# A two-block transformer forward pass on one core: the opening stages in another order

## The chip, the core and the metric

The kernel runs on one core of a Trainium2 chip. TensorE (PE) multiplies matrices into PSUM, VectorE (DVE) and ScalarE (ACT) read PSUM and on-chip memory (SBUF), GpSimd (POOL) reads and writes SBUF alone, and SyncE (SP) issues the DMAs. Each engine runs its own instructions in order and waits on semaphores for the others. The metric is the device time of one execution, in microseconds (us).

## The reference, cut to what matters

The reference computes four transformer layers on x (256 tokens by 1024 features). The first uses differential attention together with an attention over 256 rows of `mem`; the second uses block attention and again an attention over `mem`; two layers of another kind (stick-breaking and forgetting attention, with convolutional feed-forwards) follow. The change touches only the opening: the normalised memory times its key and value weights, and the first layer's projection of x.

```python
def _rmsnorm(x, g):
    y = x * lax.rsqrt(jnp.mean(x * x, axis=-1, keepdims=True) + EPS)
    return y * g
# layer a
z  = _rmsnorm(x, a_norm_attn) @ a_w_in           # v, q, k and the memory's queries
kv = _rmsnorm(mem, a_mem_norm) @ a_w_mem_kv      # mem_a: keys and values, 512 wide
# layer b
kv = _rmsnorm(mem, b_mem_norm) @ b_w_mem_kv      # mem_b: the same memory, other gain and weights
```

The scale of a row, rsqrt(mean square), is the same for mem_a and mem_b. It commutes with the product, so the kernel multiplies by the gain before the matmul and by the scale after it.

## The kernel before, in words

Every product is done at float32 accuracy from two float32r parts of each operand, a high and a low one, with three matmuls: high by high, low by high, high by low. Weights come in units of 128 by 1024 floats (512 KB), through four slots of `raw`. For each unit SP loads the slot, ACT writes its high part (`split`, line 815), DVE its low part (`split`, line 1128), and PE then does 24 matmuls of 256 columns or 12 of 512. SP may load a slot again when DVE has split it; ACT may write a slot's high part again when PE is done with its unit. The operand (x or memory) gets its high part from ACT (`high`, line 819) and its low part from DVE (`low`, line 1172), in eight pieces.

The mean square of an operand is made of eight squares on ACT (`squared`, line 827, two buffers in turn), eight additions on POOL (line 1497), a product with a matrix of ones on PE (`mean_square`, line 544; with `columns` also lines 549 to 550), and a logarithm and an exponential on ACT (`norm_scale`, lines 901 to 905). A square waits until POOL has taken the one two before it. `MS_AFTER` names the unit behind which PE and ACT place it.

The head of the kernel has these stages, in PE's order: matmuls on zeros that keep PE busy (`keep_warm`, line 559; each float32 one counts as two in the records); the four units of `mem_a` (keys and values of layer a's memory) into PSUM banks 0 to 3; the six units of `values("in_a")`, four of width 512 (group 0, banks 0 and 1) and two of width 256 (group 1, banks 2 and 3); the transposes of the two memory value tiles (line 568); and `fused("in_a")`, in which each projected tile (line 467) alternates with attention. In PE's order the mean square of the memory stands behind the third unit of mem_a, that of x behind the third unit of in_a. `mem_b`'s four units run at the end of the fused stage, from an operand that is made at the start (`h2_hi`, `h2_lo`).

On DVE, `take` (line 1164) multiplies mem_a's tiles by the scale as it moves them from PSUM to `ZM`; it comes behind the low parts of mem_a, three splits, the low parts of mem_b and of x, and the fourth split. `values("in_a")` on PE waits until these tiles are out (line 437), and for all nine constants (line 695). On SP the constants and `w_f` (the weights of a gate of the last layer) are issued between x and the first unit of in_a (lines 415 to 418).

Of the kernel before, what the change touches and what calls it, by code (L numbers as in the profile page):

```python
# [22 lines left out]
P = 128  # L23
D = 1024
TOK = 256
# [87 lines left out]
def build_program(nc, ins, out):  # L113
# [6 lines left out]
    with ctx:  # L120
# [52 lines left out]
        with ExitStack() as mlp:  # L173
# [36 lines left out]
        mem_in = sem("mem_in")  # L210
# [9 lines left out]
        rstd_kept = sem("rstd_kept")  # L220
# [56 lines left out]
        OPERANDS = {"mem_a": (0, 1), "mem_b": (8, 1), "in_a": (16, 1), "up_a": (24, 1), "in_b": (32, 2),  # L277
# [8 lines left out]
            ["mem_a", "in_a", "up_a", "in_b", "up_b", "final", "in_sb", "post_sb", "up_sb", "post_ffn_sb",  # L286
# [3 lines left out]
        MS_AFTER = {"mem_a": 2, "in_a": 2, "up_a": 1, "in_b": 2, "up_b": 1, "in_sb": 3, "up_sb": 2, "in_fox": 3,  # L290
# [80 lines left out]
        def _(sp):  # L371
            sp.dma_start(gains[:], ins["gains"]).then_inc(mem_in, 16)
            sp.dma_start(ZM[:], ins["mem"]).then_inc(mem_in, 16)
# [26 lines left out]
            for name in order:  # L400
                g = plan[name]
                nk, body = len(g["ks"]), g["body"]
                if nk == 1 and any(g["unit"] <= unit < g["unit"] + g["units"] for unit in rotations):
                    for s in range(g["units"]):
                        unit = g["unit"] + s
                        load(g, s, 0, unit - RING + 1, s % RING)
                        if unit in rotations:
                            rotate(*rotations[unit])
                elif g["trips"] == 1:
                    for s in range(body):  # L410
                        load(g, s, 0, g["unit"] + s - RING + 1 if g["unit"] else None, s % RING)
                    if name == "mem_a":
                        sp.dma_start(ones[:], ins["ones"]).then_inc(ones_in, 16)
                        sp.dma_start(X[:], ins["x"]).then_inc(x_in, 16)
                        for dst, const in CONSTS:
                            sp.dma_start(dst[:], ins[const]).then_inc(consts_in, 16)
                        sp.dma_start(H[:, 0:KT // 2, :].rearrange("p a (b c) -> p (a b) c", c=P),
                                     ins["w_f"]).then_inc(wf_in, 16)
# [11 lines left out]
        def _(pe):  # L430
            n_ms, n_vt = [0], [0]

            def values(name):
# [3 lines left out]
                pe.wait_ge(tile_out, g["tile"])  # L437
                for s, (group, _, width, k_tiles) in enumerate(value_units(name)):
                    pe.wait_ge(lo_ready, g["unit"] + s + 1)
# [12 lines left out]
                    if s == MS_AFTER[name]:  # L452
                        mean_square(columns=True)

# [238 lines left out]
            keep_warm(log_ms, 20)  # L693
            gemm("mem_a", a_hi, a_lo)
            pe.wait_ge(consts_in, 16 * len(CONSTS))
            values("in_a")
            transpose_values(ZM, 2, 2)

# [101 lines left out]
        def _(act):  # L800
# [91 lines left out]
            def norm_scale(columns=False):  # L892

                act.wait_ge(ms_done, n_norm[0] + 1)
                if n_norm[0] == NORMS["in_a"]:
                    act.wait_ge(tile_out, plan["in_a"]["tile"])
                    act.wait_ge(rstd_kept, 1)
# [7 lines left out]
                nc.scalar.activation(rstd[:], log_ms[:], ACT.Exp, scale=-0.5).then_inc(rstd_ready, 1)  # L905
# [13 lines left out]

            def values(name, middle=None):  # L920
# [3 lines left out]
                for s, (group, first, width, k_tiles) in enumerate(units):  # L924
                    split(0, RING, g["unit"] + s + RING, KT)
                    if s == MS_AFTER[name]:
                        norm_scale(columns=True)
                    if k_tiles.stop == KT:
# [120 lines left out]
            act.wait_ge(mem_in, 32)  # L1049
            for k in range(KT):  # L1050
                high("mem_a", ZM, a_hi, 0, 0, k)
            for u in range(RING):
                split(0, RING, u, KT)
                for k in (2 * u, 2 * u + 1):
                    squared("mem_a", ZM[:, k, :], 0, 0, k)
                    high("mem_b", ZM, h2_hi, 0, 0, k)
# [4 lines left out]
            project("mem_a", middle=norm_scale)  # L1061
            for k in range(KT):
                squared("in_a", X[:, k, :], 0, 0, k)
# [48 lines left out]
        def _(dve):  # L1112
# [24 lines left out]
            def query_key_tile(name, s):  # L1137
# [7 lines left out]
                if memory >= 0:  # L1145
                    dve.wait_ge(rstd_kept, 1)
# [4 lines left out]
            def values(name):  # L1151

                g = plan[name]
                for s in range(g["values"]):
                    split(0, RING, g["unit"] + s + RING - 1, KT)

            def take(name, norm, dst, shift=0):

                per = plan[name]["body"]

                def tile(i, done, b, first):
                    dve.wait_ge(units_done, done)
                    dve.wait_ge(rstd_ready, NORMS[norm] + 1)
# [526 lines left out]
```

## Time and profile before

| what | value |
|---|---|
| time, median of 3 runs | 1336.09 us (1330.67 to 1338.53) |
| the profiled execution: its own time | 1337.67 us |
| the profiled execution: its span | 1335.9 us |
| mean granted clock of TensorE | 0.966 of full speed |
| PE busy | 1246.4 us (93%) |
| DVE, ACT, POOL busy | 947.2, 734.2, 477.9 us |

### The profile page before, as it was taken

The numbers are of one execution on the slowest core, as the hardware profiler recorded it, in microseconds if no ns is written. First come the engines' busy times: TensorE is split into PE (matmuls) and PEld (weight loads), VectorE is DVE, ScalarE is ACT, GpSimd is POOL, SyncE is SP. The second block draws the span as 40 slices with busy tenths as digits, with TensorE's granted clock in tenths as the row PEclk, the third lists the DMA queues.
The fourth block names the chain that finished last, engine by engine and source line by source line (L and its number), as shares of the span: only waits on it lengthen the run. The fifth ranks groups of instructions, "written<-read, shape, count | busy, mean of one in ns | idle before, by whom it ended". The sixth has DMA issues, their size and how long they took to land. (4 is left out here: it accounts for less than half of the span.)

```text
span 1335.9 us, 29554 instructions
## 1 busy us (share of the span) xinstructions
PE 1246.4 (93%) x9952; PEld 1177.5 (88%) x9952; DVE 947.2 (71%) x1545; ACT 734.2 (55%) x1307; POOL 477.9 (36%) x465
## 2 busy tenths in 40 slices
PE   7988999999997999999997889998999999899896
PEld 7977999999985999999885779998979978899896
DVE  6598677656597677545699479997475756899844
ACT  6556554444554555444656566665465556666642
POOL 2231255300022355210222258885130004888711
PEclk9999899999998999999998799999989989999998
DMA  7544365566543456656443225555645433555472
GB/s 273 174 143 127 111 205 189 178 196 204 177 142 96 157 189 192 202 188 190 157 127 111 82 93 179 173 182 151 186 136 174 127 95 112 158 181 171 141 207 85
DMA packets 63287, 212.40 MB, mean 159 GB/s; under 512 B 7793, under 2 KB 8945, under 8 KB 62833
## 3 DMA queue, kind: packets, MB, share of 16 engines
q1 hardware_dynamic: 63216, 211.50, 50.3%
q8 instruction: 39, 0.64, 0.2%
q14 instruction: 32, 0.25, 0.1%
HBM read 207.28 MB, written 1.05 MB: 156 GB/s over the span
## 5 line engine op out<-in xcount | busy, mean ns | idle before, releaser
L1128 DVE TENSOR_TENSOR w_lo<-raw,w_hi 128x1024 fp32r<-128x1024 f32 (+2 forms) x408 | 508.9, 1253 | 144.8 <-ACT w_hi L815 144.8
L815 ACT CAST w_hi<-raw 128x1024 fp32r<-128x1024 f32 (+2 forms) x408 | 408.2, 1004 | 251.6 <-PE bank L499 166.3
L497 PE MATMUL bank<-h_hi,w_hi 128*128 128x256 f32 x1168 | 328.6, 281 | 12.2 <-DVE w_lo L1128 11.3
L498 PE MATMUL bank<-h_lo,w_hi 128*128 128x256 f32 x1168 | 324.0, 277 | 0.0
L499 PE MATMUL bank<-h_hi,w_lo 128*128 128x256 f32 x1168 | 323.9, 277 | 0.0
L1497 POOL TENSOR_TENSOR sumsq<-sumsq,square 128x256 f32<-128x256 f32 x107 | 95.6, 893 | 471.5 <-ACT square L827 287.2
L497 PE MATMUL bank<-a_hi,w_hi 128*128 128x256 f32 x896 | 251.3, 281 | 11.0 <-DVE w_lo L1128 9.3
L498 PE MATMUL bank<-a_lo,w_hi 128*128 128x256 f32 x896 | 250.5, 280 | 0.0
L499 PE MATMUL bank<-a_hi,w_lo 128*128 128x256 f32 x896 | 250.4, 279 | 0.0
L497 PEld LDWEIGHTS bank<-h_hi,w_hi 128*128 128x128 f32 x1168 | 220.2, 189 | 19.3 <-issue 18.6
L499 PEld LDWEIGHTS bank<-h_hi,w_lo 128*128 128x128 f32 x1168 | 220.4, 189 | 0.0
L498 PEld LDWEIGHTS bank<-h_lo,w_hi 128*128 128x128 f32 x1168 | 220.1, 188 | 0.1
L497 PEld LDWEIGHTS bank<-a_hi,w_hi 128*128 128x128 f32 x896 | 170.4, 190 | 12.4 <-DVE w_lo L1128 10.1
L498 PEld LDWEIGHTS bank<-a_lo,w_hi 128*128 128x128 f32 x896 | 170.4, 190 | 0.0
L499 PEld LDWEIGHTS bank<-a_hi,w_lo 128*128 128x128 f32 x896 | 169.8, 190 | 0.0
L467 PE MATMUL bank<-h_hi,w_hi 128*128 128x256 f32 x512 | 147.6, 288 | 0.0
L468 PE MATMUL bank<-h_lo,w_hi 128*128 128x256 f32 x512 | 143.3, 280 | 0.0
L469 PE MATMUL bank<-h_hi,w_lo 128*128 128x256 f32 x512 | 143.1, 280 | 0.0
L1541 POOL TENSOR_TENSOR prod<-H 128x256 f32<-128x256 f32 x64 | 89.2, 1393 | 84.8 <-DVE H L1203 84.8
L467 PEld LDWEIGHTS bank<-h_hi,w_hi 128*128 128x128 f32 x512 | 97.4, 190 | 5.1 <-issue 4.9
L1555 POOL TENSOR_TENSOR H<-H,conv_sb 128x256 f32<-128x256 f32 x88 | 97.1, 1103 | 9.8 <-DVE H L1226 7.7
L469 PEld LDWEIGHTS bank<-h_hi,w_lo 128*128 128x128 f32 x512 | 97.2, 190 | 0.0
(154 smaller groups left out, 2123.6 us busy)
## 6 DMA issues: line engine op xcount, KB each, us to landing
raw<-in_w_up_sb SPq DMA_DIRECT2D x44, 512.0 KB, 3.4
raw<-in_w_up_fox SPq DMA_DIRECT2D x44, 512.0 KB, 3.4
raw<-in_w_up_a SPq DMA_DIRECT2D x32, 512.0 KB, 3.4
raw<-in_w_down_a SPq DMA_DIRECT2D x32, 512.0 KB, 4.7
raw<-in_w_up_b SPq DMA_DIRECT2D x32, 512.0 KB, 3.4
raw<-in_w_down_b SPq DMA_DIRECT2D x32, 512.0 KB, 4.4
raw<-in_w_in_sb SPq DMA_DIRECT2D x24, 512.0 KB, 3.6
raw<-in_w_in_fox SPq DMA_DIRECT2D x24, 512.0 KB, 4.3
```

The source lines that it names most:

```text
L467: nc.tensor.matmul(dst, w_hi[:, slot, w], src_hi[:, k, :], start=k == 0, stop=False)
L468: nc.tensor.matmul(dst, w_hi[:, slot, w], src_lo[:, k, :], start=False, stop=False)
L469: last = nc.tensor.matmul(dst, w_lo[:, slot, w], src_hi[:, k, :], start=False, stop=k == KT - 1)
L497: nc.tensor.matmul(dst, w_hi[:, slot, w], src_hi[:, at + k, :], start=begin, stop=False)
L498: nc.tensor.matmul(dst, w_hi[:, slot, w], src_lo[:, at + k, :], start=False, stop=False)
L499: last = nc.tensor.matmul(dst, w_lo[:, slot, w], src_hi[:, at + k, :], start=False, stop=end)
L815: nc.scalar.copy(w_hi[:, slot, 0:k * P], raw[:, slot, 0:k * P]).then_inc(hi_ready, 1)
L1128: nc.vector.tensor_tensor(w_lo[:, slot, 0:k * P], raw[:, slot, 0:k * P], w_hi[:, slot, 0:k * P].bitcast(f32), ALU.subtract).then_inc(lo_re ...
L1497: nc.gpsimd.tensor_tensor(sumsq[:], sumsq[:], square[:, b, :], ALU.add).then_inc(sum_done, 1)
L1541: nc.gpsimd.tensor_tensor(prod[:, b % 2, :], u_buf[:, b, :], u_buf[:, b, :], ALU.mult).then_inc(prod_ready, 1)
L1555: nc.gpsimd.tensor_tensor(m_buf[:, b % 2, :], u_buf[:, b % 2, :], conv[:, layer, 0, bass.ds(i * 4 + b, 1)].broadcast_to([P, TOK]), ALU.mul ...
```

## The change

The loads: `mem` comes in two DMAs of half its pieces, with a semaphore each. The nine constants are issued behind the load of the third unit of in_a (unit 6 of the stream, s == 2), and w_f behind the fifth (s == 4), no longer ahead of the first.

ACT and DVE start on the first half of the memory alone, and split the first weight unit after six of the eight pieces. The squares of the memory and the operand of mem_b move from the start to the middle of `values("in_a")` (`opening`). The squares of x are done ahead of `values("in_a")`, between splits, and x's mean square is the first on PE, behind the second unit of in_a. The memory's mean square follows behind the fifth.

mem_a's four tiles are copied from PSUM to `Z` as they are (`take_memory`). They are multiplied by the memory's scale at the end of `values("in_a")`, from SBUF to SBUF, and PE's transposes wait for that (`mem_scaled`). `values("in_a")` on PE waits for two tiles to be out, and for four in its second group. `keep_warm` makes 16 matmuls and not 20. `norm_scale` writes the memory's scale straight to `rstd_mem`, and the copy of it goes. The new semaphores' declarations are left out here, and so are unchanged lines:

```diff
@@ -274,7 +275,7 @@
-        OPERANDS = {"mem_a": (0, 1), "mem_b": (8, 1), "in_a": (16, 1), "up_a": (24, 1), "in_b": (32, 2),
+        OPERANDS = {"mem_a": (0, 1), "in_a": (8, 1), "mem_b": (16, 1), "up_a": (24, 1), "in_b": (32, 2),
                     "q_b": (33, 2), "up_b": (48, 1), "in_sb": (56, 1), "up_sb": (64, 1), "in_fox": (72, 2),
@@ -283,11 +284,11 @@
         NORMS = {n: i for i, n in enumerate(
-            ["mem_a", "in_a", "up_a", "in_b", "up_b", "final", "in_sb", "post_sb", "up_sb", "post_ffn_sb",
+            ["in_a", "mem_a", "up_a", "in_b", "up_b", "final", "in_sb", "post_sb", "up_sb", "post_ffn_sb",
              "in_fox", "post_fox", "up_fox", "post_ffn_fox"])}
-        MS_AFTER = {"mem_a": 2, "in_a": 2, "up_a": 1, "in_b": 2, "up_b": 1, "in_sb": 3, "up_sb": 2, "in_fox": 3,
+        MS_AFTER = {"in_a": 1, "up_a": 1, "in_b": 2, "up_b": 1, "in_sb": 3, "up_sb": 2, "in_fox": 3,
                     "up_fox": 2}
@@ -369,8 +370,10 @@
         def _(sp):
-            sp.dma_start(gains[:], ins["gains"]).then_inc(mem_in, 16)
-            sp.dma_start(ZM[:], ins["mem"]).then_inc(mem_in, 16)
+            sp.dma_start(gains[:], ins["gains"]).then_inc(gains_in, 16)
+            for h in range(2):
+                part = slice(h * KT // 2, (h + 1) * KT // 2)
+                sp.dma_start(ZM[:, part, :], ins["mem"][:, part, :]).then_inc(mem_in[h], 16)
             def load(g, f, part, free, slot):
@@ -406,16 +409,18 @@
                             rotate(*rotations[unit])
+                        if name == "in_a" and s == 2:
+                            for dst, const in CONSTS:
+                                sp.dma_start(dst[:], ins[const]).then_inc(consts_in, 16)
+                        if name == "in_a" and s == 4:
+                            sp.dma_start(H[:, 0:KT // 2, :].rearrange("p a (b c) -> p (a b) c", c=P),
+                                         ins["w_f"]).then_inc(wf_in, 16)
                 elif g["trips"] == 1:
...
                         sp.dma_start(X[:], ins["x"]).then_inc(x_in, 16)
-                        for dst, const in CONSTS:
-                            sp.dma_start(dst[:], ins[const]).then_inc(consts_in, 16)
-                        sp.dma_start(H[:, 0:KT // 2, :].rearrange("p a (b c) -> p (a b) c", c=P),
-                                     ins["w_f"]).then_inc(wf_in, 16)
                 else:
@@ -434,8 +439,11 @@
                 g = plan[name]
-                pe.wait_ge(tile_out, g["tile"])
+                if name != "in_a":
+                    pe.wait_ge(tile_out, g["tile"])
                 for s, (group, _, width, k_tiles) in enumerate(value_units(name)):
+                    if name == "in_a" and k_tiles.start == 0:
+                        pe.wait_ge(tile_out, 2 * group + 2)
                     pe.wait_ge(lo_ready, g["unit"] + s + 1)
@@ -451,6 +459,8 @@
                         mean_square(columns=True)
+                    if name == "in_a" and s == 4:
+                        mean_square()
             def query_key_tile(name, s, src_hi, src_lo):
@@ -690,11 +700,13 @@
             pe.wait_ge(warm_ready, 1)
-            keep_warm(log_ms, 20)
+            keep_warm(log_ms, 16)
             gemm("mem_a", a_hi, a_lo)
...
             values("in_a")
+            pe.wait_ge(mem_scaled, 4)
             transpose_values(ZM, 2, 2)
+            pe.wait_ge(h_lo, operand_count("mem_b", 0, 0, KT - 1))
             fused("in_a", lambda s: query_key_tile("in_a", s, *((h1_hi, h1_lo) if s < 2 + 2 * ROPE_PAIRS
@@ -892,9 +904,7 @@
                 act.wait_ge(ms_done, n_norm[0] + 1)
-                if n_norm[0] == NORMS["in_a"]:
-                    act.wait_ge(tile_out, plan["in_a"]["tile"])
-                    act.wait_ge(rstd_kept, 1)
+                dst = rstd_mem if n_norm[0] == NORMS["mem_a"] else rstd
                 if columns:
@@ -902,7 +912,7 @@
                 link(nc.scalar.activation(log_ms[:], bank[7][:, 0:TOK], ACT.Ln, scale=1.0 / D, bias=eps_col[:]))
-                nc.scalar.activation(rstd[:], log_ms[:], ACT.Exp, scale=-0.5).then_inc(rstd_ready, 1)
+                nc.scalar.activation(dst[:], log_ms[:], ACT.Exp, scale=-0.5).then_inc(rstd_ready, 1)
                 n_norm[0] += 1
@@ -916,6 +926,17 @@
                     squared(norm, X[:, k, :], 0, 0, k)
+
+            def opening(s):
+
+                if s == 0:
+                    for k in range(KT):
+                        high("mem_b", ZM, h2_hi, 0, 0, k)
+                elif s in (1, 2):
+                    for k in range(4 * (s - 1), 4 * s):
+                        squared("mem_a", ZM[:, k, :], 0, 0, k)
+                elif s == 4:
+                    norm_scale()
             def values(name, middle=None):
@@ -925,6 +946,8 @@
                         norm_scale(columns=True)
+                    if name == "in_a":
+                        opening(s)
                     if k_tiles.stop == KT:
@@ -1046,21 +1069,26 @@
             nc.scalar.preload_act_table_set("natural_log_exp_and_others")
-            act.wait_ge(mem_in, 32)
-            for k in range(KT):
+            act.wait_ge(gains_in, 16)
+            act.wait_ge(mem_in[0], 16)
+            for k in range(4):
                 high("mem_a", ZM, a_hi, 0, 0, k)
-            for u in range(RING):
+            act.wait_ge(mem_in[1], 16)
+            for k in (4, 5):
+                high("mem_a", ZM, a_hi, 0, 0, k)
+            split(0, RING, 0, KT)
+            for k in (6, 7):
+                high("mem_a", ZM, a_hi, 0, 0, k)
+            for u in range(1, RING):
                 split(0, RING, u, KT)
-                for k in (2 * u, 2 * u + 1):
-                    squared("mem_a", ZM[:, k, :], 0, 0, k)
-                    high("mem_b", ZM, h2_hi, 0, 0, k)
             act.wait_ge(x_in, 16)
...
             act.wait_ge(a_ready, RING)
-            project("mem_a", middle=norm_scale)
-            for k in range(KT):
-                squared("in_a", X[:, k, :], 0, 0, k)
+            for u in range(RING):
+                for k in (2 * u, 2 * u + 1):
+                    squared("in_a", X[:, k, :], 0, 0, k)
+                split(0, RING, RING + u, KT)
             values("in_a")
@@ -1143,27 +1171,22 @@
                 if memory >= 0:
-                    dve.wait_ge(rstd_kept, 1)
                     dst, scale = ZM[:, 4 + memory, :], rstd_mem
...
                 split(0, RING, unit + RING - 1, KT)
-            def values(name):
+            def values(name, after_second=None):
                 g = plan[name]
-                for s in range(g["values"]):
+                for s in range(len(value_units(name))):
                     split(0, RING, g["unit"] + s + RING - 1, KT)
-
-            def take(name, norm, dst, shift=0):
-
-                per = plan[name]["body"]
-
-                def tile(i, done, b, first):
-                    dve.wait_ge(units_done, done)
-                    dve.wait_ge(rstd_ready, NORMS[norm] + 1)
-                    nc.vector.tensor_tensor(dst[:, i * per + (shift + b), :], bank[b][:, 0:TOK], rstd[:],
-                                            ALU.mult).then_inc(tile_out, 1)
-                return tile
+                    if s == 1 and after_second is not None:
+                        after_second()
+
+            def take_memory(u):
+
+                dve.wait_ge(units_done, u + 1)
+                nc.vector.tensor_copy(Z[:, 8 + u, :], bank[u][:, 0:TOK]).then_inc(tile_out, 1)
             def low(name, src, dst_hi, dst_lo, i, per, k):
@@ -1392,18 +1415,26 @@
             nc.vector.memset(eps_col[:], EPS).then_inc(a_ready, RING)
-            for k in range(KT):
+            for k in range(6):
                 low("mem_a", ZM, a_hi, a_lo, 0, 0, k)
-            for u in range(RING - 1):
+            split(0, RING, 0, KT)
+            for k in (6, 7):
+                low("mem_a", ZM, a_hi, a_lo, 0, 0, k)
+            for u in range(1, RING):
                 split(0, RING, u, KT)
             for k in range(KT):
-                low("mem_b", ZM, h2_hi, h2_lo, 0, 0, k)
-            for k in range(KT):
                 low("in_a", X, h1_hi, h1_lo, 0, 0, k)
-            dve.wait_ge(h_lo, 2 * KT)
-            project("mem_a", before=take("mem_a", "mem_a", ZM))
-            nc.vector.tensor_copy(rstd_mem[:], rstd[:]).then_inc(rstd_kept, 1)
-            values("in_a")
+            for u in range(RING):
+                take_memory(u)
+                if u:
+                    split(0, RING, RING - 1 + u, KT)
+            values("in_a", lambda: [low("mem_b", ZM, h2_hi, h2_lo, 0, 0, k) for k in range(KT)])
+            dve.wait_ge(rstd_ready, NORMS["mem_a"] + 1)
+            dve.wait_ge(h_lo, operand_count("mem_b", 0, 0, KT - 1))
+            dve.wait_ge(tile_out, RING)
+            dve.wait_ge(sum_done, 2 * KT)
+            for u in range(RING):
+                nc.vector.tensor_tensor(ZM[:, u, :], Z[:, 8 + u, :], rstd_mem[:], ALU.mult).then_inc(mem_scaled, 1)
             dve.wait_ge(consts_in, 16 * len(CONSTS))
@@ -1570,8 +1601,8 @@
                     trip(i, False)
+            sum_squares("in_a")
             sum_squares("mem_a")
-            sum_squares("in_a")
             pool.wait_ge(consts_in, 16 * len(CONSTS))
```

## Rows read from the trace of the kernel before

**Rows 1.** The page: busy time and share of one engine.
```profile
PE 1246.4 (93%) x9952; PEld 1177.5 (88%) x9952; DVE 947.2 (71%) x1545; ACT 734.2 (55%) x1307; POOL 477.9 (36%) x465
```

**Rows 2.** Windows of the head: stretch, length, busy of five engines, clock, DMA share, GB/s.
```profile
6.00:9.00 3.00, 3.00 (x16) 2.64 (x15) 2.17 (x6) 2.71 (x7) 0.00 (x0) 1.00 1.01 412
...
18.00:21.00 3.00, 3.00 (x27) 2.89 (x25) 3.00 (x5) 2.94 (x8) 1.86 (x3) 1.00 0.99 400
...
26.30:31.50 5.20, 4.58 (x24) 4.40 (x25) 3.80 (x8) 0.93 (x3) 0.00 (x0) 0.67 0.74 221
```

**Rows 3.** Timeline of PE: start, us, engine, line, operation, tiles, count, idle before.
```profile
1.20 11.18 PE L559 MATMUL bank<-log_ms 128*128 128x256 f32 x40 [1.20 <-DVE log_ms L1393]
12.03 0.47 PE L497 MATMUL bank<-a_hi,w_hi 128*128 128x256 f32 x1
...
20.70 0.59 PE L544 MATMUL bank<-sumsq,ones_sb 128*128 128x256 f32 x2
26.37 0.58 PE L497 MATMUL bank<-a_hi,w_hi 128*128 128x256 f32 x1 [5.08 <-DVE w_lo L1128]
...
31.51 0.47 PE L447 MATMUL bank<-w_hi,h_hi 128*128 128x512 f32 x1 [0.56 <-issue]
...
40.25 0.70 PE L544 MATMUL bank<-sumsq,ones_sb 128*128 128x256 f32 x2 [0.24 <-POOL sumsq L1497]
...
49.65 0.60 PE L568 MATMUL bank<-ident_sb,ZM 128*128 128x128 f32 x4
```

**Rows 4.** Timeline of DVE, head of the kernel.
```profile
16.82 5.19 DVE L1172 SCALAR_TENSOR_TENSOR h_lo<-ZM,gains_sb,h_hi 128x256 fp32r<-128x256 f32 x8
21.94 3.24 DVE L1172 SCALAR_TENSOR_TENSOR h_lo<-X,gains_sb,h_hi 128x256 fp32r<-128x256 f32 x8
25.11 3.48 DVE L1128 TENSOR_TENSOR w_lo<-raw,w_hi 128x1024 fp32r<-128x1024 f32 x3
```

**Rows 5.** Timeline of ACT, head of the kernel.
```profile
19.13 3.29 ACT L819 ACTIVATE h_hi<-X,gains_sb 128x256 fp32r<-128x256 f32 x8
...
38.78 2.92 ACT L815 CAST w_hi<-raw 128x1024 fp32r<-128x1024 f32 x3
41.62 0.25 ACT L901 ACTIVATE log_ms_col<-bank,eps_col 128x2 f32<-128x2 f32 x1
...
42.50 0.42 ACT L905 ACTIVATE rstd<-log_ms 128x256 f32<-128x256 f32 x1
...
45.20 1.26 ACT L932 ACTIVATE v_tok<-bank,rstd_col 128x512 f32<-128x512 f32 x2
```

**Rows 6.** Timeline of SP, issues of DMAs.
```profile
1.68 2.37 SPq L380 DMA_DIRECT2D raw<-in_w_mem_a  x4
...
4.61 0.45 SPq L414 DMA_DIRECT2D X<-in_x  x1
...
9.08 0.44 SPq L416 DMA_DIRECT2D b_f_sb<-in_b_f  x1
```

**Rows 7.** DMAs: size and time from issue to landing; the first is unit 0's.
```profile
raw<-in_w_mem_a SPq DMA_DIRECT2D x1, 512.0 KB, 5.9
X<-in_x SPq DMA_DIRECT2D x1, 1024.0 KB, 9.6
b_f_sb<-in_b_f SPq DMA_DIRECT2D x1, 0.5 KB, 10.8
```

**Rows 8.** Timeline of POOL in the head, and the additions' least, median and longest ns.
```profile
10.99 9.16 POOL L1497 TENSOR_TENSOR sumsq<-sumsq,square 128x256 f32<-128x256 f32 x8 [9.93 <-ACT square L827]
32.54 7.66 POOL L1497 TENSOR_TENSOR sumsq<-sumsq,square 128x256 f32<-128x256 f32 x8 [10.87 <-issue]
L1497 POOL TENSOR_TENSOR sumsq<-sumsq,square x16: 737/741/1539, 11.0 to 39.5; 128x256 f32<-128x256 f32 x16
```

**Rows 9.** PE's windows behind two waits of 2.1 us: stretch, length, busy, clock, DMA, GB/s.
```profile
800.00:803.00 3.00, 2.68 (x15) 0.69 0.50 153
1143.00:1146.00 3.00, 2.72 (x23) 1.00 0.53 157
```

More of the change, by code:

```diff
@@ L209, in build_program @@
         x_in = sem("x_in")
-        mem_in = sem("mem_in")
+        gains_in = sem("gains_in")
+        mem_in = [sem(f"mem_in{h}") for h in range(2)]
+        mem_scaled = sem("mem_scaled")
         raw_in = [sem(f"raw_in{s}") for s in range(RING)]
@@ L219, in build_program @@
         rstd_ready = sem("rstd_ready")
-        rstd_kept = sem("rstd_kept")
         col_ready = sem("col_ready")
```

## The prediction, made before the changed kernel had run

> **What bounds the kernel now.** The page comes first: PE is busy for 93% of the span and the next engine, DVE, for 71% [rows 1]. So the question for a change of order is which waits of PE it takes out of the chain, and which it puts in. The change ends at the transposes of the memory's values: from there on both kernels issue the same work on PE in the same order. Those transposes start at 49.65 us [rows 3], and I forecast the time by when they start afterwards.
>
> PE's own timeline shows where those 49.65 us go. PE runs matmuls on zeros until 12.03, then three units of mem_a until 20.70, which is 2.89 us a unit. After the mean square it stands idle for 5.08 us, until the fourth unit's low part is written at 26.3. It takes up that unit at 26.37 and starts the values at 31.51, behind the eviction of the scaled tiles. There the mean square of x waits only 0.24 us, and the values run on to 49.65: 9.40 us from that mean square for three units, of which it takes 0.9 itself, so 2.83 us a unit [rows 3]. DVE's timeline gives the reason for the idle time: the low parts of mem_b (5.19 us) and of x (3.24 us) stand ahead of the fourth split, which begins at 25.11 [rows 4]. A second loss hides behind it. In the window from 26.3 to 31.5 the granted clock is 0.67, so PE ran a part of it at 1.2 GHz after that idle time; 5.2 us at 0.67 are 1.7 us lost [rows 2]. Idle time, lost clock and the eviction make 7 to 8 us, and that is all that a better order can win.
>
> **The start.** Four matmuls on zeros go, eight records. In the window from 6 to 9 us 16 records take 3.00 us, 0.19 us each [rows 2], so PE is free 1.5 us earlier, at 10.5. By their mean, 11.18 us over 40 [rows 3], it would be 2.2 us. The weights have to be there: unit 0 is issued at 1.68 and lands 5.9 us later, at 7.6 [rows 6, 7]. ACT's split takes 0.97 us (a third of 2.92) [rows 5] and DVE's 1.16 us (a third of 3.48) [rows 4], so it is ready at 9.8, since six pieces of the memory are enough ahead of it. The two halves of the memory serve this. They cost SP one more issue, about 0.5 us, which its long queue hides; without that cover units 0 to 3 would come 0.5 us later. The four units then follow each other, since mem_b's operand is no longer ahead of their splits: 10.5 + 4 x 2.89 = 22.1.
>
> **The constants.** This is the new wait. PE still waits for all nine ahead of the values, and they now queue on SP and in the DMA engines behind units 4, 5 and 6. x lands at 4.61 + 9.6 = 14.2 and b_f, the last constant, at 9.08 + 10.8 = 19.9 [rows 6, 7]: the constants took 5.7 us behind x. Three units of 512 KB at 400 GB/s [rows 2] take 1.31 us each, so the last lands at 14.2 + 3.9 + 5.7 = 23.8. I take this value, since it keeps the queue in order and uses the constants' own row. The lower bound is no wait at all (22.1). The upper is the latency itself: unit 6 may be issued when unit 2 is split, near 13.1, nine issues of 0.49 us bring b_f to 17.5, and 10.8 us more give 28.3. So PE waits from 22.1 to 23.8, with everything else at hand: x's high parts are ready at 14.2 + 3.3 = 17.5 [rows 5], its low parts at 18.1, and unit 4 is split by 20.5 behind two copies of mem_a's tiles. Unscaled eviction itself costs DVE no more than before, and takes the scale off this path.
>
> **x's mean square.** Its squares and additions start at 17.5 between splits. In that form the eight additions took 9.16 us [rows 8], so they end at 27. PE wants them behind two value units, at 23.8 + 5.7 = 29.5. The wait is nothing, with 2.5 us of cover; with that gone each microsecond would be on the path. With 0.9 us for the mean square and three more units (8.5) PE comes to the memory's mean square at 38.9.
>
> **The memory's mean square.** ACT is the chain here. Unit 4 is done at 26.7, so the split of unit 8 ends at 27.6. The eight high parts of mem_b take 3.3 us (as x's did [rows 5]): 30.9. The split of unit 9 gives 31.9, x's scale, 1.3 us (41.62 to 42.92 [rows 5]), gives 33.2. Then come the squares. In the form in which POOL sets the pace, eight additions took 7.66 us, after 0.55 us for the first square [rows 8]: 41.4. The bounds are 6.1 us (eight at 0.76) and 12.3 us (eight at the longest, 1.54) [rows 8]. So PE waits from 38.9 to 41.4, 2.5 us, and everything behind it in PE's queue waits too: the sixth unit, the transposes, the first projected tile. With 0.6 us for the mean square and one unit it is through at 44.8.
>
> The Trainium skill has a rule against this part: SBUF — State Buffer, "Who interferes with whom", says that a VectorE instruction with two SBUF inputs holds up a GpSimd instruction that reads SBUF. The rows fit it, with additions between 737 and 1539 ns; by the median alone the chain would end 1.6 us earlier than by the 7.66 us, by the longest 4.6 us later (rival D).
>
> **The scaling.** The last square ends about 1.4 us ahead of the last addition, at 40.0. ACT then has a split (41.0), the eviction of the first values, 1.26 us [rows 5] (42.2), a split (43.2), and the memory's scale, 0.9 us (44.1). DVE splits until 44.4 and makes four products of 128x256 at 0.40 us, the price of x's low parts (3.24 over 8 [rows 4]): 46.0. The transposes wait for this, so they start at 46.0, 3.65 us earlier than before.
>
> **The clock.** PE waits twice for about 2 us. Behind two waits of 2.1 us later in this trace the clock was 0.69 once and 1.00 once [rows 9]. I take it that the wait of 2.5 us brings it down and that of 1.7 us doesn't. A fall costs up to 1.7 us [rows 2], but PE has 1.2 us to spare between 44.8 and 46.0, so 0.6 us are on the path.
>
> **The rest.** w_f moves behind unit 8 and is wanted by ACT only after the transposes; it costs nothing, and if it were late it would hold the fused stage's first DVE work. The order of the operands and of the norms changes counts only, and the copy of the scale (0.29 us on DVE) goes from a place that nobody waits for.
>
> **The sum.** 3.65 - 0.6 = 3.0 us less. The profiled execution took 1337.67 us, 1.8 us more than its span and 1.6 us over the median: 1334.7 for it, and 1336.09 - 3.0 = 1333.1 us by the median of the runs. Of the 7 to 8 us in the head about 4.5 come back as the waits for constants, for POOL and for the scaling.
>
> **The rivals.** A: the constants are there when PE wants them (b_f's 4 bytes a partition may have been held by w_f, which was issued right behind it and now isn't). PE starts the values 1.7 us earlier and all that follows moves with it: 1331.4; with additions at 0.76 us too it would be 1329.4. For it speaks that the other constants came sooner; against it that the queue ahead is the longer by 1.5 MB.
>
> B: the clock falls at the wait for constants as well. Then 1.7 us are lost ahead of everything: 1334.8. For it speaks the 0.69 behind 2.1 us, against it the 1.00.
>
> C, the other side: the constants are late. If b_f keeps 10.8 us from its issue, the values start at 28.3 instead of 23.8, 4.5 us later, and after a wait of 6.2 us the clock falls, as it did behind 5.08 us: 1333.1 + 4.5 + 1.7 = 1339.3. It decides from where the values start 3.0 us later than I say, at 26.8, or with the fallen clock at 25.1. Against it: 10.8 us was mostly the queue ahead, which by 17.5 is nearly empty.
>
> D: the additions for the memory run at POOL's longest. They end 4.6 us later, all on PE's path: 1337.7. Against it: DVE has only two splits in that stretch.
>
> E: the 3 us are given back later, in the fused stages where PE waits for other engines: 1336.1. For it speaks the spread of the three runs, 7.9 us, which is more than all I forecast.
>
> **How the numbers follow.** My forecast 0.40, A 0.20, B 0.14, C 0.07, D 0.06, E 0.13. A measurement of this kernel can tell about 0.5%, 6.7 us. Faster by more than that is below 1329.4: the fast end of A (0.10), and scatter around my own case (0.06), 0.16 in all. Slower by more, above 1342.8, would need C or D with scatter: 0.05. Within: 0.79. The range reaches from A's fast end, with a little scatter, to between D and C: 1328.5 to 1338.0.
>
> **What would show it.** PE's first weight matmul near 10.5; no gap between units of mem_a; a gap ahead of line 447's first matmul with a DMA of a constant as releaser, ending near 23.8; a gap of about 2.5 us ahead of the second mean square (line 544's successor), released by POOL; transposes near 46. I am wrong if PE's gaps sum to well under 4 us there (then A or better), or if the transposes come early and the total doesn't move (E).

## The result

The changed kernel takes 1329.55 us, the median of 20 runs; the kernel before takes 1333.07 us, the median of 20 runs that include its three shown above. The ratio is 0.9971, with a 95% interval of 0.9958 to 0.9984: 3.5 us less by the medians, 2.1 to 5.6 by the interval. I had forecast 3.0 us less. The forecast time, 1333.1, was made against a median of three runs that lay 3 us above the median of twenty, so it is the difference that was right.

The page of the kernel after, which answers to [rows 1]:

```profile
span 1326.3 us, 29540 instructions
...
PE 1235.6 (93%) x9944; PEld 1166.7 (88%) x9944; DVE 949.7 (72%) x1548; ACT 733.7 (55%) x1307; POOL 479.7 (36%) x465
```

PE's timeline of the kernel after, to be read against [rows 3]; the bracket is the idle time ahead and who ended it:

```profile
1.21 8.65 PE L569 MATMUL bank<-log_ms 128*128 128x256 f32 x32 [1.21 <-DVE log_ms L1416]
10.63 0.39 PE L507 MATMUL bank<-a_hi,w_hi 128*128 128x256 f32 x1 [0.78 <-DVE w_lo L1156]
...
22.25 0.50 PE L455 MATMUL bank<-w_hi,h_hi 128*128 128x512 f32 x1 [0.44 <-DMA b_f_sb<-in_b_f]
28.80 0.70 PE L554 MATMUL bank<-sumsq,ones_sb 128*128 128x256 f32 x2 [0.78 <-POOL sumsq L1528]
41.63 1.12 PE L554 MATMUL bank<-sumsq,ones_sb 128*128 128x256 f32 x2 [3.35 <-POOL sumsq L1528]
46.57 0.60 PE L578 MATMUL bank<-ident_sb,ZM 128*128 128x128 f32 x4
```

The one wait of 5.08 us is gone. The transposes start at 46.57 against 49.65 before, 3.08 us earlier (forecast: 46.0, and 0.6 for the clock). By PE's own timeline the 3.08 us are three parts: its first unit starts 1.40 us earlier; the waits between there and the transposes are 4.57 us (0.44, 0.78, 3.35) where they were 5.88 (5.08, 0.56, 0.24); and the work between takes 0.37 us less. This is an account and not a price: e12 below takes back a half of the earlier start, and the head hardly feels it.

Three timelines of the kernel after, ACT's, DVE's and POOL's, where they make the chain in front of the memory's mean square and of the transposes:

```profile
27.65 3.30 ACT L831 ACTIVATE h_hi<-ZM,gains_sb 128x256 fp32r<-128x256 f32 x8
30.85 1.03 ACT L827 CAST w_hi<-raw 128x1024 fp32r<-128x1024 f32 x1
...
33.00 0.71 ACT L839 ACTIVATE square<-ZM 128x256 f32<-128x256 f32 x2
...
43.73 0.42 ACT L915 ACTIVATE rstd_mem<-log_ms 128x256 f32<-128x256 f32 x1
```

```profile
44.50 1.43 DVE L1437 TENSOR_TENSOR ZM<-Z,rstd_mem 128x256 f32<-128x256 f32 x4
```

```profile
18.64 10.11 POOL L1528 TENSOR_TENSOR sumsq<-sumsq,square 128x256 f32<-128x256 f32 x8 [17.59 <-ACT square L839]
33.53 3.79 POOL L1528 TENSOR_TENSOR sumsq<-sumsq,square 128x256 f32<-128x256 f32 x4 [3.31 <-issue]
37.48 4.10 POOL L1528 TENSOR_TENSOR sumsq<-sumsq,square 128x256 f32<-128x256 f32 x4 [0.17 <-ACT square L839]
```

The high parts of mem_b, a split and x's scale stand ahead of the memory's first square on ACT.

The two spans differ by 9.6 us, three times what the head gives. Summed over windows of 5 us from 0 to 1315, the time lost to a clock below full, (1 - granted clock) x 5 us, is 40.9 us in the trace before and 32.5 in the one after, and 1.7 in the head of both. So 8.4 us of lost clock, of which a part fell on PE's idle time, differ after the head, where the two kernels are the same. The 20 runs of either spread over 9 to 11 us.

### The profile page after: what moved, and what is told of

It is laid out like the page before. It is cut to its first block and busy times, and to the rows that moved or that the text cites. A ratio compares the mean times of both kernels' runs of the same rounds, so it can differ in the third digit from the quotient of the medians.

```text
span 1326.3 us, 29540 instructions
## 1 busy us (share of the span) xinstructions
PE 1235.6 (93%) x9944; PEld 1166.7 (88%) x9944; DVE 949.7 (72%) x1548; ACT 733.7 (55%) x1307; POOL 479.7 (36%) x465
## 5 line engine op out<-in xcount | busy, mean ns | idle before, releaser
L509 PE MATMUL bank<-h_hi,w_lo 128*128 128x256 f32 x1168 | 323.7, 277 | 0.0
L509 PE MATMUL bank<-a_hi,w_lo 128*128 128x256 f32 x896 | 248.1, 277 | 0.0
L509 PEld LDWEIGHTS bank<-h_hi,w_lo 128*128 128x128 f32 x1168 | 219.5, 188 | 0.0
L509 PEld LDWEIGHTS bank<-a_hi,w_lo 128*128 128x128 f32 x896 | 168.9, 188 | 0.0
```

The source lines that it names most:

```text
L509: last = nc.tensor.matmul(dst, w_lo[:, slot, w], src_hi[:, at + k, :], start=False, stop=end)
```

## The experiments

A landmark serves for the head, since it stands out from the scatter of the total: ACT's first softmax exponential, in the second stage, at 64.07 us before and at 61.00 in the kernel after.

```profile
64.07 0.51 ACT L965 ACTIVATE p_buf<-s_buf,unit_bias 128x256 f32<-128x256 f32 x1 [1.38 <-DVE unit_bias L1306]
```

```profile
61.00 0.51 ACT L988 ACTIVATE p_buf<-s_buf,unit_bias 128x256 f32<-128x256 f32 x1 [1.39 <-DVE unit_bias L1329]
```

It has a scatter of its own. From the first projected tile to the landmark it is 14.07 us in the kernels before and after and in e9, and 13.66 to 13.69 in e1, e4 to e8, e11 and e12, where the code of that stretch is the same (last section). So 0.4 us of a difference between the two groups is not the edit's. "Ratio" is the ratio of the time to the kernel before's, with its 95% interval; it rests on 12 runs, or 6 for e2 and e10. e5 to e8 are one execution each, under the profiler, and have no ratio.

**e1: the changed kernel again.**

> The changed kernel once more, beside the kernel before on one chip, as the base for the others of this group. My theory (the gain is what the head gives: the transposes start 3.1 us earlier, and nothing else is different): the transposes start at 46.6 us within 0.3, and the ratio to before is near 0.997 to 0.998. Rival (most of the 9.6 us between the two profiled spans comes from the change): the ratio is near 0.993.

Ratio 0.9983 (0.9968 to 0.9997), transposes at 47.72, landmark at 61.75. The ratio is what I expected; the transposes are 1.1 us later than I gave. The constants landed 1 us later (23.2, not 22.2), but the memory's mean square moved by 0.24 us only. The rest came behind it, from the clock. Windows of PE alone (stretch, length, busy, clock, DMA share, GB/s) in the kernel after, then in e1, then in e8, in which the wait is filled:

```profile
39.00:42.00 3.00, 0.37 (x1) 0.96 0.56 175
42.00:45.00 3.00, 3.00 (x14) 0.50 0.46 124
45.00:48.00 3.00, 3.00 (x27) 0.97 0.67 228
```

```profile
39.00:42.00 3.00, 0.13 (x1) 0.75 0.54 175
42.00:45.00 3.00, 3.00 (x12) 0.50 0.37 138
45.00:48.00 3.00, 3.00 (x19) 0.61 0.60 217
```

```profile
39.00:42.00 3.00, 3.00 (x15) 1.00 0.51 175
42.00:45.00 3.00, 3.00 (x25) 1.00 0.35 117
45.00:48.00 3.00, 2.18 (x20) 1.00 0.69 232
```

**e8 and e11: the wait filled.** e8 is one execution, e11 the same kernel over 12 runs.

```diff
                     if name == "in_a" and s == 4:
+                        keep_warm(ones, 8)
                         mean_square()
```

> The changed kernel with 8 matmuls on ones (about 3.0 us) on PE just ahead of the memory's mean square, in the stretch where it waits 3.35 us. It tells what the clock's fall cost there. My theory (the sixth unit ran mostly at 1.2 GHz, 4.4 us in place of 2.83, and 1.1 of the 1.6 us were hidden by the scaling on DVE): the granted clock stays at 1.00, the sixth unit ends near 45.0, the transposes start at 45.9 to 46.1, 0.6 us earlier. Rival (PE's clock is the path there): the transposes start 1.5 us earlier, at 45.0.

> The changed kernel with 8 matmuls on ones ahead of the memory's mean square once more, now timed: in one look the transposes started at 46.1 against 46.6 and 47.7 without the filling. My theory (the filling saves between 0.6 us and 1.6 us in the head, by how late the constants were, and nothing later): ratio to before 0.996 to 0.998, as the changed kernel's. Rival (keeping the clock up there also spares falls later in the kernel, as the one look at 1321.7 us may say): ratio below 0.995.

```profile
46.12 0.66 PE L579 MATMUL bank<-ident_sb,ZM 128*128 128x128 f32 x4 [0.82 <-DVE ZM L1438]
```

In e8 the transposes start at 46.12, released by DVE, and the landmark is at 60.20. The constants ended their wait at 23.09, as in e1 at 23.24, and against e1 the filling gives 1.6 us, all that the fall took; against the kernel after, whose constants came at 22.25, it gives 0.45. In e11 they start at 45.77; ratio 0.9965 (0.9948 to 0.9981). The clock stayed at 1.00 in both heads, while it fell behind this wait in the kernel after, e1, e5 and e12. So the fall goes with PE's idle time here (e6, below, is an exception). The rival is not borne out, since the ratio is not below 0.995, though its interval reaches there. The profiled span of e11 was 1334.7 us with 39.2 us of lost clock, all of it behind the head, and that of e8 1319.9 us with 27.8.

**e5: w_f right behind the constants** (its DMA moved from s == 4 to the loop's end at s == 2).

> The changed kernel with w_f issued right behind the last constant, as before, in place of behind unit 8. It tells why b_f landed at 22.2 and 23.2 in the changed kernel and not at my 23.8. Theory of rival A (w_f behind it in the queue held b_f's landing by 2 us): b_f lands 1.5 to 2.4 us later than in the changed kernel, at 24 to 25.5, and the values start there. The other theory (the small transfers take less time behind whole weight units; w_f is no matter): b_f lands at 22.2 to 23.3 as without this edit.

```profile
22.47 0.50 PE L454 MATMUL bank<-w_hi,h_hi 128*128 128x512 f32 x1 [0.79 <-DMA b_f_sb<-in_b_f]
```

In this one execution w_f does not hold b_f by the 1.5 to 2.4 us that rival A needs. In six traces PE waits for b_f ahead of the values, and they start between 22.25 and 23.24; in e11 they start at 22.56 without a wait. The reason that I gave for rival A falls, though the constants did come earlier than I took.

**e6: constants and w_f in their old place on SP** (both loops moved back behind `X`).

> The changed kernel with the constants and w_f issued in their old place, ahead of in_a's first unit. My theory (the queue is one line, so what is put first only changes who waits): the constants are in by 20, but unit 4 lands at 22.4 as before and its split takes until 24.7, so the values start at 24.7 and not at 22.2 to 23.2, and the transposes move by the same 1.5 to 2.5 us. Rival (ACT and POOL set the start of the second half anyway): the values start later but the transposes stay at 46.6 to 47.7.

```profile
22.53 1.04 ACT L825 CAST w_hi<-raw 128x1024 fp32r<-128x1024 f32 x1 [3.52 <-DMA raw<-in_w_in_a]
...
25.09 0.47 PE L453 MATMUL bank<-w_hi,h_hi 128*128 128x512 f32 x1 [3.11 <-DVE w_lo L1154]
45.09 0.70 PE L552 MATMUL bank<-sumsq,ones_sb 128*128 128x256 f32 x2 [3.35 <-POOL sumsq L1526]
49.44 0.66 PE L576 MATMUL bank<-ident_sb,ZM 128*128 128x128 f32 x4 [0.83 <-DVE ZM L1435]
```

ACT waits 3.52 us for unit 4, now behind 1.5 MB of constants and w_f, and splits it at 22.53; in the kernel after it did so at 18.71. The values start at 25.09, the transposes at 49.44 (46.57 in the kernel after, 47.72 in e1) and the landmark is at 63.51. The first projected tile starts at 49.85 against 50.00 in the kernel before. So in this order the later loads of the constants and w_f, undone together, carry nearly the whole gain of the head; how much of it each carries I did not try. The clock fell behind the wait of 3.11 us (0.51 from 27 to 30), and then not behind the one of 3.35, which made up for a part of the delay.

**e7: mem_b's operand at the start again,** behind the four splits and ahead of x's on ACT and DVE.

> The changed kernel with mem_b's operand made at the start again, behind the four splits and ahead of x's, on both ACT and DVE. My theory (in the new order DVE's low parts of mem_b are no longer ahead of a split that PE wants, and moving them to the middle put 3.3 us on ACT ahead of the memory's squares, so this part of the change is worth nothing): the values start 1 to 2 us later, the memory's squares start at once behind x's scale, and the transposes are within 0.7 us of the changed kernel's. Rival (the late operand is what freed the head): the wait of 5 us comes back and the transposes are at 49 or later.

```profile
23.78 0.47 PE L455 MATMUL bank<-w_hi,h_hi 128*128 128x512 f32 x1 [0.96 <-DVE w_lo L1155]
...
41.88 0.70 PE L554 MATMUL bank<-sumsq,ones_sb 128*128 128x256 f32 x2 [1.36 <-POOL sumsq L1529]
46.23 0.66 PE L578 MATMUL bank<-ident_sb,ZM 128*128 128x128 f32 x4 [0.82 <-DVE ZM L1438]
```

The values start later, PE's wait for the memory's sum shrinks from 3.35 to 1.36 us, and the landmark is at 60.31, 0.7 us earlier than in the kernel after. Of these 0.7 us, 0.3 are there at the first projected tile, and 0.4 are the other pace behind it (last section), so I don't call it better. In the new order, making this operand later is worth nothing, by this one execution.

**e12: 20 matmuls on zeros.**

> The changed kernel with 20 matmuls on zeros at the start as before, in place of 16. My theory (PE takes up the first unit 1.3 to 1.5 us later, at 12.0, but 0.4 to 0.9 us of that are only waited for the constants behind mem_a; the rest moves everything): first unit at 12.0, values at 23.3 to 23.6 where units take 2.83 us (23.0 where they take 2.72), transposes 0 to 1.2 us later than in the changed kernel, ratio to before 0.997 to 0.999. Rival (PE's start is the path and all of it comes back): transposes 1.4 us or more later.

```profile
23.13 0.50 PE L455 MATMUL bank<-w_hi,h_hi 128*128 128x512 f32 x1 [0.15 <-DMA b_f_sb<-in_b_f]
...
46.74 0.60 PE L578 MATMUL bank<-ident_sb,ZM 128*128 128x128 f32 x4
```

First unit at 11.32 (10.63 in the kernel after), values at 23.13 after a wait of 0.15 us for b_f, transposes at 46.74, landmark at 60.75, ratio 0.9974 (0.9957 to 0.9992); one of the 12 runs, of 4250 us, is not in it. The start is not on the path. I had the first unit 0.7 us too late: PE was through with the zeros earlier.

**e3 and e9: the kernel before, with mem_b's operand made later, alone.** In both, mem_a's scaled tiles go to `Z`, and the memory stays in `ZM`. e3 makes the operand behind the fifth and sixth value unit and waits for it ahead of the fused stage:

```diff
-            dve.wait_ge(h_lo, 2 * KT)
-            project("mem_a", before=take("mem_a", "mem_a", ZM))
+            project("mem_a", before=take("mem_a", "mem_a", Z, 8))
...
+            pe.wait_ge(h_lo, operand_count("mem_b", 0, 0, KT - 1))
```

> The kernel before with one part of the change alone: the operand of mem_b is made behind the value units in place of at the start (mem_a's tiles are scaled on eviction as before, but go to Z and are read there, since the memory must stay). My theory (the 5.08 us of idle time were DVE's low parts of mem_b ahead of the fourth split, and nothing else in the old order costs much): no wait of PE above 1 us inside mem_a, transposes at 43.5 to 45 against 49.65 before and 46.6 in the changed kernel, ratio to before 0.995 to 0.997. Rival (the whole new order is needed: x's mean square would come late, or the units of in_a): the transposes start at 46.6 or later.

```profile
24.08 0.38 PE L497 MATMUL bank<-a_hi,w_hi 128*128 128x256 f32 x1 [3.09 <-DVE w_lo L1131]
...
47.40 0.60 PE L568 MATMUL bank<-ident_sb,Z 128*128 128x128 f32 x4
50.36 0.38 PE L467 MATMUL bank<-h_hi,w_hi 128*128 128x256 f32 x1 [2.36 <-DVE h_lo L1178]
```

Ratio 1.0013 (0.9998 to 1.0029): I missed. A wait of 3.09 us is left inside mem_a, where x's low parts are still ahead of the fourth split, and my own wait for mem_b's low parts took what was won behind it. The clock fell behind that wait too (0.80 and 0.63 from 50 to 56 us), and the landmark is at 65.66, later than before. e9 makes the operand sooner, behind x's scale, and waits for them only at mem_b's tiles:

> The kernel before with mem_b's operand made behind x's scale (high parts on ACT behind the third value unit, low parts on DVE behind the fourth), and waited for on PE only at mem_b's own tiles. The earlier form made PE wait 2.36 us for the low parts ahead of the first projected tile, which took all of the gain back. My theory: that wait is gone, the first projected tile starts at 47.5 to 48.2 against 50.0 before, ratio to before 0.997 to 0.999. Rival (taking mem_b out of the start doesn't help in the old order, because another wait takes its place): 49.5 or later and a ratio of 1.000.

The first projected tile starts at 47.98, the landmark is at 62.05 (2.0 us earlier than before) and the ratio is 0.9981 (0.9965 to 0.9997). So in the old order this one part is worth 2 us, where in the new order it is worth none.

**e4: the old order of mean squares with the new loads** (e3, the changed kernel's SP, 16 matmuls on zeros, and DVE's fourth split ahead of x's low parts).

> The kernel before with mem_b's operand behind the value units, and with the changed kernel's loads: memory in two DMAs, six pieces ahead of the first split, 16 matmuls on zeros, constants behind unit 6, w_f behind unit 8; the fourth split of DVE ahead of x's low parts. The memory's mean square stays the first, and its tiles are scaled on eviction. My theory (putting x's mean square first brings nothing and makes the late chain of square, sum, scale and product that PE waits for): values start at 22.3 to 23.8, transposes at 41 to 42.5, ratio to before 0.993 to 0.995. Rival (ACT and POOL can't do both sets of squares by the third value unit): a wait of 2 us or more ahead of x's mean square, transposes at 44 or later.

```profile
22.76 2.35 DVE L1145 TENSOR_TENSOR w_lo<-raw,w_hi 128x1024 fp32r<-128x1024 f32 x2
25.03 1.42 DVE L1184 TENSOR_TENSOR Z<-bank,rstd 128x256 f32<-128x256 f32 x4
```

```profile
26.55 0.47 PE L452 MATMUL bank<-w_hi,h_hi 128*128 128x512 f32 x1 [2.79 <-DVE Z L1184]
...
47.63 0.38 PE L472 MATMUL bank<-h_hi,w_hi 128*128 128x256 f32 x1 [2.35 <-DVE h_lo L1192]
```

The values start at 26.55, behind the scaled eviction (2.79 us), and the same wait of 2.35 us for mem_b's operand as in e3 stands ahead of the first tile, at 47.63. Landmark 61.32, ratio 0.9980 (0.9962 to 0.9999). I missed this too. The eviction holds the values back, but the trace doesn't say that the scale does: the scale is there at 24.93, and DVE is through with the splits ahead of the eviction at 25.1. And the transposes start at 44.68, 1.89 us before those of the kernel after. So the old order of mean squares, with the new loads and without that last wait, which e9 takes out, might be ahead of the new one. That form I did not run.

**e2: the transposes behind two projected tiles.**

```diff
-                    if name == "in_a" and s == 4:
+                    if name == "in_a" and s == 5:
                         mean_square()
...
-            pe.wait_ge(mem_scaled, 4)
-            transpose_values(ZM, 2, 2)
...
+                query_key_tile("in_a", s, *((h1_hi, h1_lo) if s < 2 + 2 * ROPE_PAIRS else (h2_hi, h2_lo)))
+                if s == 1:
+                    pe.wait_ge(mem_scaled, 4)
+                    transpose_values(ZM, 2, 2)
```

> The changed kernel with the memory's mean square on PE behind the sixth value unit, and the transposes of the memory's values (and ACT's copy of them) behind the first two projected tiles. My theory (PE has 3.35 us and then nothing to spare behind the memory's squares, and only the transposes need the scale): the wait ahead of the mean square shrinks from 3.35 us to about 0.5, the first projected tile starts at about 42.3 in place of 46.9, the third at 48.8 to 49.6 in place of 52.6, and the total is 3 to 4 us below the changed kernel's (ratio to before 0.994 to 0.995). Rival (ACT and DVE are the chain there, so PE waits for them a little later instead): the third projected tile starts at 51.5 or later, and the total is the changed kernel's.

```profile
41.74 0.70 PE L554 MATMUL bank<-sumsq,ones_sb 128*128 128x256 f32 x2 [0.80 <-POOL sumsq L1532]
42.63 0.36 PE L477 MATMUL bank<-h_hi,w_hi 128*128 128x256 f32 x1 [0.18 <-ACT v_tok L959]
48.36 0.60 PE L578 MATMUL bank<-ident_sb,ZM 128*128 128x128 f32 x4
```

The chain on ACT and POOL ends where it did (41.7), but PE has work meanwhile, and the scaling on DVE is hidden. Landmark 56.94, 4.1 us earlier than in the kernel after; ratio 0.9944 (0.9926 to 0.9963). This confirms that in the kernel after the memory's sum and scale are the path.

**e10: both chains started sooner.** Besides e2's edit, x's squares go between its high parts, the memory's squares ahead of mem_b's high parts, and waits go to where the thing is used:

```diff
-            for k in range(KT):
+            for k in (0, 1):
                 high("in_a", X, h1_hi, 0, 0, k)
...
+                if u < RING - 1:
+                    for k in (2 * u + 2, 2 * u + 3):
+                        high("in_a", X, h1_hi, 0, 0, k)
                 split(0, RING, RING + u, KT)
```

> The form with the late transposes, and more: x's squares on ACT between its high parts, the memory's squares ahead of mem_b's high parts (one square, one high part, in turn), mem_b's low parts at the end of the value units, PE's wait for the constants and for mem_b's operand where each is used, and the lambda and w_f work of DVE behind the second projected tile. My theory (the two chains square, add, scale are started too late, not too slow): no wait of PE above 1 us for x's mean square or the memory's, first projected tile at 40.3 to 41.5 against 42.6, third at 46.4 to 47.5 against 48.7, ratio to before 0.992 to 0.9935. Rival (POOL's additions beside DVE's low parts are what lasts, so an earlier start is eaten by contention): the wait ahead of x's mean square grows over 1.5 us and the first projected tile is at 42 or later.

```profile
10.69 0.38 PE L507 MATMUL bank<-a_hi,w_hi 128*128 128x256 f32 x1 [0.18 <-DVE w_lo L1162]
40.05 0.36 PE L477 MATMUL bank<-h_hi,w_hi 128*128 128x256 f32 x1 [0.44 <-DVE w_lo L1162]
46.45 0.63 PE L578 MATMUL bank<-ident_sb,ZM 128*128 128x128 f32 x4 [0.71 <-DVE ZM L1450]
```

Those are all of PE's waits from the first unit to there. The landmark is at 55.16, 8.9 us earlier than before, and the ratio 0.9918 (0.9895 to 0.9942), 1321.59 us by the median of 6 runs. It is the fastest form that I ran, and its interval lies below that of the kernel after (0.9958 to 0.9984).

## Why the prediction was right, step by step

Rows for what follows: ACT's timeline in the kernel after, then in e1, and b_f's DMA in the kernel after (size, us from issue to landing).

```profile
14.88 3.31 ACT L831 ACTIVATE h_hi<-X,gains_sb 128x256 fp32r<-128x256 f32 x8 [1.75 <-DMA X<-in_x]
...
25.76 1.99 ACT L827 CAST w_hi<-raw 128x1024 fp32r<-128x1024 f32 x2
```

```profile
15.07 3.31 ACT L831 ACTIVATE h_hi<-X,gains_sb 128x256 fp32r<-128x256 f32 x8 [1.75 <-DMA X<-in_x]
```

```profile
b_f_sb<-in_b_f SPq DMA_DIRECT2D x1, 0.5 KB, 4.2
```

- **The start.** I said 10.5, it was 10.63, but by another reason. The zeros ended 0.78 us before; the last to come was the low part of unit 0, at 10.58 and not at 9.8 (ACT split it at 8.27 and DVE at 9.35). In e1 the zeros took longer, 9.72 us and not 8.65, and PE went on from them without a wait, at 10.82. e12 adds 0.7 us there and the transposes move by 0.2.
- **The constants.** The wait was there, with b_f as releaser, but ended at 22.25 (e1: 23.24) and not at 23.8. SP issued b_f at 18.05, and it landed 4.2 us later (5.0 in e1), which is far from the 10.8 us of rival C. I had said that all that follows moves with it, which was wrong: 1 us more in e1 moved the memory's mean square by 0.24 us, and 0.19 of these were there before the constants, since ACT took up x at 15.07 and not at 14.88. From there ACT has no wait for PE in either trace until the memory's squares are done. So rival A's earlier constants came true in part, without its gain. Rival A's fast end was also added up wrongly: 1331.4 less 1.6 is 1329.8, and not 1329.4.
- **x's mean square.** I had no wait with 2.5 us of cover. It was 0.78 us: the additions began at 18.64 and not at 17.5, they took 10.11 us where I took 9.16, and PE came 1.5 us earlier, at 28.0.
- **The memory's mean square.** I had 2.5 us of wait, ending at 41.4, by ACT's queue; it was 3.35 us, ending at 41.63. The high parts of mem_b began at 27.65, where I had 27.6, and this is luck. I let ACT wait there for PE to be done with unit 4, at 26.7. PE was done by 25.3, and ACT came late by its own queue: x's squares, in which it waits for POOL, and the splits between them. Eight additions and the gap between them took 8.05 us. I took 7.66 [rows 8], near enough, and nothing like rival D's. The 0.76 us an addition in my lower bound is not in [rows 8]; by the median there, 0.741, the bound is 5.9 us and not 6.1.
- **The scaling.** 46.0 forecast; DVE's four products end at 45.93.
- **The clock.** I said that the second wait brings it down and the first doesn't, and that 0.6 us of it are on the path. In the kernel after it is so: the sixth unit ran until 46.5, and the transposes begin at 46.57 and not at 45.9. In e1 the fall costs 1.6 us, since the clock stays down longer: 0.75, 0.50 and 0.61 in the three windows shown, against 0.96, 0.50 and 0.97 in the same windows of the kernel after. Rival B, a fall at the first wait too, is seen in no trace in which PE waits for the constants; but those waits were of 0.15 to 1.16 us, and not of 1.7, so its question was not put.
- **The rest (rival E).** Not given back: the median moved by 3.5 us, and the interval (2.1 to 5.6) leaves out nought.

So the sum was right, and partly by luck. The term of the constants was 1.6 us too long, and the chain behind it hung on x's landing and ACT's queue and not on the constants: two errors that cancel in one chain. The forecast of 3.0 us is also finer than the head repeats: the same code gave 3.08 us at the transposes once and 1.93 the other time (e1). I had also left open which part of the change brings the gain. The runs say: the later constants and w_f together nearly all of it (e6, an undo, one execution); fewer zeros nothing (e12); mem_b's operand nothing in this order (e7). The two halves of the memory, and x's mean square first, I did not try alone.

## What to carry to other kernels

Ask of each wait not how long it is but whose chain it ends: here 1 us more of one did not move the chain that set the end, and filling another with useful work (two projected tiles that don't need the scale) gave 4.1 us in the head. A part's worth belongs to its order: mem_b's operand later gave 2 us in the old order and nothing in the new. When a chain alternates between two engines, start it earlier by interleaving it with what it was queued behind, and put PE's wait at the first use, as in e10.

## What the runs showed of the hardware

At a granted clock of 1.00 the same stream of matmuls ran at either of two paces. From one L509 to the L509 two triples on, in mem_a's units, first the kernel after, then e1:

```profile
19.83 0.28 PE L509 MATMUL bank<-a_hi,w_lo 128*128 128x256 f32 x1
...
20.51 0.28 PE L509 MATMUL bank<-a_hi,w_lo 128*128 128x256 f32 x1
```

```profile
20.00 0.28 PE L509 MATMUL bank<-a_hi,w_lo 128*128 128x256 f32 x1
...
20.70 0.28 PE L509 MATMUL bank<-a_hi,w_lo 128*128 128x256 f32 x1
```

That is 0.113 us and 0.117 us a matmul, 2.72 and 2.83 us a unit, with nothing in the code or the clock's record to tell them apart. The stages change places: in the kernel after the first units are the quick ones and the projected tiles the slow ones (evictions at 55.69 and 58.52, 2.83 us apart), in e1 it is the other way (56.54 and 59.27, 2.73). Together with the falls of the clock, it makes up the scatter of single runs that I can name. The falls don't follow from the length of a wait alone: they came after some waits of 2.1 us and not after others [rows 9], and after 3.35 us in the kernel after (0.50 from 42 to 45) but not after 3.35 us in e6 (1.00 from 42 to 51). The Trainium skill (TensorE: Matmul & The Clock Gate, "Wait — 56ns, not 53.3ns?") gives the start-to-start time at full clock as columns over 2.4 GHz and 2.5 ns. By that formula I estimate 109 ns for 256 columns. The quick pace lies 4 ns above it, and the slow one is not in the page. What sets the pace stays open.
